# Attention heads in pairs on TensorE, and a weight ring of two slots beside them

## The chip, the core and the metric

The kernel runs on one NeuronCore of a Trainium2 chip, in one launch. The core has a matrix engine (TensorE; PE in the profile, with its weight loads as PEld), a vector engine (DVE), an activation engine (ACT), a general engine (POOL), a queue engine that here only issues DMA transfers (SP), an on-chip memory of 128 partitions (SBUF) and eight accumulator banks of 128 x 512 f32 (PSUM) that TensorE writes. The metric is the device time of one execution in microseconds. Three runs of the kernel before took 1537.32, 1537.51 and 1539.07 us (median 1537.51).

## The reference, cut to what matters

Two blocks in a row on a 512 x 1024 activation. The first mixes the sequence (a recurrence and a Fourier transform), then runs 16 experts. The second, whose middle is what changes here, is this:

```
h = rms_norm(x, norm_gain)
q, k, v, z_a, u, z_s, g_a, g_s = split(h @ w_in)         # 512 columns each, g_a and g_s 1024
g_a, g_s = g_a + gate_bias[:1024], g_s + gate_bias[1024:]
y_a = band_attention(q, k, v, rel_bias)                  # 8 heads of 64, chunk of 64, 8 chunks back
y_a = (y_a * silu(z_a)) @ w_attn_out
y_s = s5_ssm(u, ...)                                     # 32 groups, 64 complex states each
...                                                      # gelu, a gated linear unit, * silu(z_s), @ w_ssm_out
x = x + (sigmoid(g_a) * y_a + sigmoid(g_s) * y_s) @ w_out
```

With 512 positions every query sees all keys up to its own chunk, so a head is a lower triangle of 128 x 128 tiles: for the query tile q (0 to 3) the scores are 128 x 128(q+1), then bias, softmax over the row, and the product with the values.

## The kernel before, in words

Each engine has one instruction stream written out by hand; the order of the work is the order of the loops in the code, and semaphores tie the streams together. A weight matrix arrives in units of 1 MB. A unit goes through a chain: SP loads it into a slot of a ring (`load`, the slot by `slot_of`); ACT writes its rounded upper part into one of two other slots (`weights_hi`, `B2_HI`); DVE subtracts it in place, which leaves the lower part (`weights_lo`); TensorE then forms upper x lower, lower x upper and upper x upper products (`product`, `project`), and its last matmul of the unit counts up `unit_used`, which frees the slot.

The middle of the second block is a loop of `STEPS` = 12 steps `i`. Before it the units of u, q, k and v have been projected. Each step projects one unit of gate columns (two `project` calls of 24 matmuls each, into the banks of `gate{2i}` and `gate{2i+1}`). Behind them TensorE does what is left of step i, head by head, for the first `HEADS` = 8 steps:

- `head_scores(i+1)`: four matmuls with 64 rows (the head's 64 dimensions, q stationary, k moving), 384, 128, 256 and 512 columns wide. All matmuls of one head lie in the same half of the array's rows.
- `head_probs(i)`: ten transposes of 128 x 128 probability tiles through three banks.
- `ssm_out` (even steps) or `ssm_states` (odd steps): matmuls of the state space part, for group quarter c.
- `head_values(i)`: ten matmuls of 128 columns, the values stationary (64 columns, so half of the array's columns), the transposed probabilities moving.
- `ssm_tables` (even) or `ssm_lags` (odd): small matmuls for the tables of quarter c.

DVE in a step reads the score banks with scale and bias and takes the row maxima, multiplies the last head's result into `zaT`, scales the exponentials by the reciprocal sums, in even steps reads the lag rows and runs `states` (rotations and a scan), in odd steps builds `input_table`, and then makes the lower part of the next step's unit and finishes the silu of the gates. ACT takes the exponentials of head i, the upper part of the next unit, the tanh of the gates, and copies the transposed probabilities to SBUF (`pT`). POOL builds `output_table(c + 1)` as soon as `ssm_out(c)` has run, then writes y and the lag rows to memory and reads the lag rows back as `toep`, by DMAs that it issues itself.

The ring in this part has three slots (`B2_RING`, slots 4, 5 and 8); unit n waits for unit n - 3. The score banks are 0, 1 and 2, the state space banks 3, and four banks (4 to 7) take turns for gates, transposes and values. For scores of the first step the four matmuls of head 0 stand ahead of the loop.

Of the kernel before, what the change touches and what calls it, by code (L numbers as in the profile page):

```python
# [31 lines left out]
ALU = mybir.AluOpType  # L32
# [3 lines left out]
P = 128  # L36
# [16 lines left out]
HEADS, DH = 8, 64  # L53
NREL, CHUNK = 192, 64
# [26 lines left out]
B2_RING, B2_HI = (4, 5, 8), (9, 10)  # L81
MOE_END = B1_UNITS + NE * E_UNITS
# [48 lines left out]
def build(nc, x, cols_d, cst_d, wbd_d, w_in, dft_s, w_out, w_gate, w_up, w_down, gf_d, w_in2, relp,  # L131
          bc_d, w_glu, w_ao, w_so, w_out2, gfin_d, out, u_dram, y_dram, x_dram, l_dram):
    with ExitStack() as ctx:
# [91 lines left out]
        att = area("att", RING * UNIT, TT, S)  # L225
        relb = area("relb", ends["att"], HEADS, REL)
# [36 lines left out]
        ysT = kT  # L263

# [97 lines left out]
        SCORE_BANK, SSM_BANK = {3: 0, 2: 1, 1: 2}, 3  # L362
        for i in range(STEPS):
            if i == 0:
                for q in range(1, TT):
                    jobs.add(f"score0_{q}", SCORE_BANK[q])
            mine = (4, 5 + i % 2, 6 - i % 2, 7) if i < HEADS else (None,) * 4
            for n in range(2):
                jobs.add(f"gate{2 * i + n}", mine[n], M + 8 + i if n else None)
            if i + 1 < HEADS:  # L370
                for q in range(1, TT):
                    jobs.add(f"score{i + 1}_{q}", SCORE_BANK[q])
            if i < HEADS:
                for b in range(3):
                    jobs.add(f"probT{i}_{b}", mine[(2, 3, 0)[b]])
            if i % 2 == 0 and 2 <= i <= 2 * CT:
                jobs.add(f"ssm{i // 2 - 1}", SSM_BANK)
            if i % 2 == 1 and i < 2 * CT:
                jobs.add(f"state{i // 2}", SSM_BANK)
            if i < HEADS:  # L380
                jobs.add(f"pv{i}", mine[1])
            if i % 2 == 0 and i < 2 * CT:
                for n, name in enumerate(("st_re", "st_im")):
                    jobs.add(f"{name}_{i // 2}", mine[2 + n])
            if i % 2 == 1 and i < 2 * CT:
                jobs.add(f"lags_{i // 2}", mine[3])
            if i == HEADS - 1:
                jobs.turn = mine[0]
# [20 lines left out]
        def slot_of(unit):  # L409

            return unit % RING if unit < MOE_END else B2_RING[(unit - MOE_END) % RING2]

# [4 lines left out]
        def loaded(eng, unit):  # L417

            s = slot_of(unit)
            if unit < MOE_END:  # L420
                n = unit // RING + 1
            else:
                n = loads_b1[s] + (unit - MOE_END) // RING2 + 1
# [40 lines left out]
        def score_at(q):  # L464
# [1606 lines left out]
```

## Time and profile before

| | before |
|---|---|
| median of 3 runs | 1537.51 us |
| the profiled execution's own time | 1538.49 us |
| its span, first to last instruction | 1536.5 us |
| TensorE (PE) busy | 1407.3 us, 92% |
| DVE busy | 566.4 us, 37% |
| ACT busy | 315.6 us, 21% |
| POOL busy | 132.7 us, 9% |
| granted TensorE clock, mean | 0.989 of full speed |

The profile is one execution recorded on the chip. Busy time is the union of an engine's instructions; a busy TensorE need not be at its peak, since matmuls overlap and their ends are modelled. f32 matmuls are recorded as two instructions each, so that "x8" is four matmuls; transposes and the fp32r matmuls of the projections are one each. In a timeline row several instructions of one kind are merged, and the time in brackets is how long the engine was idle before the first, and for what. The experts take the span from about 220 to 1104 us; the loop of steps begins at 1210 us.

### The profile page before, as it was taken

What the parts mean: (1) busy time and instruction counts of PE and PEld (TensorE: products, weight loads), DVE (VectorE), ACT (ScalarE), POOL (GpSimd) and SP (SyncE); (2) the same over time, 40 slices, a digit from 0 to 9 for tenths busy, and PEclk for the clock granted to TensorE, in tenths of its full rate; (3) what the DMA queues carried; (4) which work ended last, traced back from release to release, by engine and by line L of the source; (5) the groups of instructions that cost most, each with busy time, mean ns of one, the idle gap of its engine ahead of it and who ended that gap; (6) DMA issues with size and microseconds to landing.
All of it is one profiled execution on the core that took longest, in us unless ns stands there. A gap on an engine that the chain in (4) does not pass through costs nothing.

```text
span 1536.5 us, 17099 instructions
## 1 busy us (share of the span) xinstructions
PE 1407.3 (92%) x6839; PEld 776.8 (51%) x6839; DVE 566.4 (37%) x1007; ACT 315.6 (21%) x501; POOL 132.7 (9%) x203
## 2 busy tenths in 40 slices
PE   7999699999998998988988988988799999999997
PEld 5878333443332332332332332333388888888875
DVE  6784501221120111111101201201389487755663
ACT  6582200010010010010000000000333333334332
POOL 1030000000000000000000000000123114451001
PEclk9999899999999999999999999999999999999999
DMA  9035599999999999999999999999755222225231
GB/s 330 1 107 222 219 390 425 428 428 428 427 428 430 429 428 428 428 430 428 428 427 429 430 427 428 428 430 429 280 176 139 83 73 79 70 88 185 83 110 55
DMA packets 67469, 465.19 MB, mean 303 GB/s; under 512 B 5472, under 2 KB 32352, under 8 KB 42720
## 3 DMA queue, kind: packets, MB, share of 16 engines
q1 hardware_dynamic: 63152, 454.71, 71.7%
q0 software_dynamic: 3984, 9.41, 2.4%
q8 instruction: 31, 0.51, 0.1%
q10 hardware_dynamic: 288, 0.45, 0.1%
q14 instruction: 14, 0.11, 0.0%
HBM read 457.76 MB, written 6.78 MB: 302 GB/s over the span
## 4 chain that ended last, share of the span: by engine, by line
PE 59%; DMA 34%; DVE 3%; ACT 2%; issue 1%; SPq 0%; POOL 0%; DVEq 0%; POOLq 0%; ACTq 0%
DMA wide<-in_w_down 23%; PE bank L788 14%; DMA early<-in_w_down 10%; PE bank L583 8%; PE bank L584 8%; PE bank L585 8%; PE bank L815 6%; PE bank L828 4%; PE bank L870 1%; PE bank L895 1%; PE bank L752 1%; PE bank L759 1%; ACT ring_r L1020 1%; DMA ring<-in_w_in 1%; PE bank L883 1%
## 5 line engine op out<-in xcount | busy, mean ns | idle before, releaser
L788 PE MATMUL bank<-wide,xinT 128*64 128x512 f32 x1376 | 306.9, 596 | 47.8 <-DMA wide<-in_w_up 26.9
L788 PEld LDWEIGHTS bank<-wide,xinT 128*64 128x64 f32 x1376 | 95.6, 137 | 257.3 <-issue 171.8
L1420 DVE SCALAR_TENSOR_TENSOR th<-th,bank 128x512 f32<-128x512 f32 x32 | 20.6, 684 | 432.8 <-ACT th L1155 432.8
L788 PE MATMUL bank<-early,xinT 128*64 128x512 f32 x672 | 150.5, 596 | 26.0 <-DMA early<-in_w_up 14.7
L815 PE MATMUL bank<-wide,actT 128*64 128x512 f32 x688 | 153.0, 594 | 3.7 <-issue 3.0
L583 PE MATMUL bank<-hT_lo,ring_r 128*128 128x512 f32 x352 | 139.9, 397 | 0.0
L585 PE MATMUL bank<-hT_hi,ring_r 128*128 128x512 f32 x352 | 137.1, 389 | 0.0
L584 PE MATMUL bank<-hT_hi,ring_r 128*128 128x512 f32 x352 | 137.1, 389 | 0.0
L1155 ACT ACTIVATE th<-bank 128x512 f32<-128x512 f32 x32 | 17.4, 595 | 516.1 <-PE bank L788 516.1
L788 PEld LDWEIGHTS bank<-early,xinT 128*64 128x64 f32 x672 | 45.9, 137 | 129.6 <-issue 79.0
L1417 DVE TENSOR_TENSOR ring_r<-ring,ring_r 128x2048 fp32r<-128x2048 f32 x38 | 88.3, 2324 | 43.5 <-ACT ring_r L1020 43.2
L815 PEld LDWEIGHTS bank<-wide,actT 128*64 128x64 f32 x688 | 55.4, 137 | 93.7 <-issue 80.0
L1417 DVE TENSOR_TENSOR xinT<-bank,cols 128x512 f32<-128x512 f32 x17 | 11.8, 691 | 223.2 <-PE bank L759 223.2
L1417 DVE TENSOR_TENSOR xres<-xres,bank 128x512 f32<-128x512 f32 x128 | 78.2, 681 | 7.5 <-PE bank L828 7.5
L1020 ACT ACTIVATE ring_r<-ring 128x2048 fp32r<-128x2048 f32 x38 | 72.5, 1910 | 33.3 <-PE bank L585 31.4
L1320 POOL TENSOR_SCALAR stat<-stat 128x1 f32<-128x1 f32 x4 | 1.3, 329 | 879.6 <-ACT hT L1175 879.5
L815 PE MATMUL bank<-early,actT 128*64 128x512 f32 x336 | 75.3, 595 | 2.1 <-issue 1.8
L583 PEld LDWEIGHTS bank<-hT_lo,ring_r 128*128 128x128 f32 x352 | 66.1, 188 | 16.2 <-issue 2.5
L584 PEld LDWEIGHTS bank<-hT_hi,ring_r 128*128 128x128 f32 x352 | 66.1, 188 | 14.3 <-issue 1.0
L585 PEld LDWEIGHTS bank<-hT_hi,ring_r 128*128 128x128 f32 x352 | 66.1, 188 | 14.0
L752 PE MATMUL bank<-nrm,sel 128*64 128x512 f32 x272 | 61.3, 592 | 0.8 <-issue 0.8
L828 PE MATMUL bank<-eo,gselT 64*128 64x512 f32 x256 | 60.8, 600 | 1.1
(336 smaller groups left out, 1705.6 us busy)
## 6 DMA issues: line engine op xcount, KB each, us to landing
wide<-in_w_gate SPq DMA_DIRECT2D x43, 2048.0 KB, 40.1
wide<-in_w_up SPq DMA_DIRECT2D x43, 2048.0 KB, 39.1
wide<-in_w_down SPq DMA_DIRECT2D x43, 2048.0 KB, 38.5
early<-in_w_gate SPq DMA_DIRECT2D x21, 2048.0 KB, 40.2
early<-in_w_up SPq DMA_DIRECT2D x21, 2048.0 KB, 39.2
early<-in_w_down SPq DMA_DIRECT2D x21, 2048.0 KB, 38.6
ring<-in_w_in SPq DMA_DIRECT2D x26, 1024.0 KB, 5.3
ring<-in_w_out SPq DMA_DIRECT2D x8, 1024.0 KB, 5.0
```

Source lines behind the costliest of these rows:

```text
L583: pe.matmul(dst, a[0], b[1], start=first, stop=False)
L584: pe.matmul(dst, a[1], b[0], start=False, stop=False)
L585: return pe.matmul(dst, a[0], b[0], start=False, stop=last)
L752: last = pe.matmul(bank[0][CAP * q:CAP * q + CAP, :], sel[:, t, :], nrm[:, t, 512 * q:512 * q + 512], start=(t == 0), stop=(t == TT - 1))
L759: last = pe.transpose(bank[0][:, j * P:(j + 1) * P], xg[:, 2 * P * (j // 2) + j % 2:2 * P * (j // 2 + 1):2], ident)
L788: last = pe.matmul(bank[1 + 2 * (m % 2) + q // 2][o:o + 64, :], xinT[:, k, :], w[:, i, q * 512:(q + 1) * 512], start=(k == 0), stop=(k == ...
L815: last = pe.matmul(bank[7][64 * n:64 * n + 64, :], actT[:, j // 2 * 4 + i, at:at + 64], w[:, i, n * 512:n * 512 + 512], start=(j == 0 and ...
L828: pe.matmul(bank[b][:, :], gselT[64 * n:64 * n + 64, t, :], eo[64 * n:64 * n + 64, :], start=True, stop=True).then_inc(bank_full[b], 1)
L1020: act_e.activation(hi_of(unit), used(unit, ring[slot_of(unit)]), ACT.Copy).then_inc(w_hi, 1)
L1155: act_e.activation(th[:, b, :], bank[1 + b][:, :], ACT.Tanh, scale=0.5).then_inc(tanh_ready, 1)
L1417: return dve.tensor_tensor(out_, a, b, op)
L1420: return dve.scalar_tensor_tensor(out_, a, s, b, op0, op1)
```

## The change

**Heads in pairs.** Heads 2p and 2p+1 are handled together. `pair_scores(p)` issues the eight score matmuls of both, alternating between the heads, so between rows 0 to 63 and rows 64 to 127 of the array; the six results that need a bank of their own go to six banks (`SCORE_TILES`). `pair_values(p)` has four matmuls per head instead of ten, 512, 384, 256 and 128 columns wide, alternating between the heads, so between the two column halves, into one bank. There is a second buffer `pT_b` for transposed probabilities, and probability tiles of the odd head lie in `att_b` and `att_c`; `att_c` and `pT_b` take the room of ring slot 8.

**Weight ring.** While slot 8 is taken, the units use only slots 4 and 5 (`B2_SLOTS`): from the unit of the sixth index on, unit n waits for unit n - 2. Slot 8 comes back at unit index 18, after the last pair's values.

**Order.** Scores of pair p+1, transposes, lags and values stand in the odd steps; tables, `ssm_out` and `ssm_states` in the even steps, in this order. DVE reads the scores of both heads and scales both in the even step, and runs `states` at the head of the odd step, its lag rows and input table at the tail. ACT makes the upper part of the next unit ahead of the exponentials in even steps, takes the eight exponentials there, and copies six pieces of transposed probabilities in the odd steps. The four reciprocals of a head are one. Banks are handed out anew. Nothing changes in what is computed.

The core of the diff (the rest is declarations and the same renaming on the other engines):

```diff
+B2_SLOTS = [4, 5, 8] * 2 + [4, 5] * 5 + [4, 5, 8] * 4 + [4, 5]
+SLOT8_BACK = 18
...
+        SCORE_TILES = [((0, 3),), ((1, 3),), ((0, 2), (0, 0)), ((1, 2), (1, 0)), ((0, 1),), ((1, 1),)]
...
-            mine = (4, 5 + i % 2, 6 - i % 2, 7) if i < HEADS else (None,) * 4
+            odd, (one, other) = i % 2, ((6, 7), (7, 6))[i // 2 % 2]
+                jobs.add(f"gate{2 * i + n}", ((5, one), (other, 5))[odd][n] if i < HEADS else None, M + 8 + i if n else None)
+                for a, b, at in ((0, 0, 0), (1, 0, 3), (0, 1, 1), (1, 1, 4), (0, 2, 2), (1, 2, other)):
+                    jobs.add(f"probT{2 * p + a}_{b}", at)
+                jobs.add(f"lags_{p}", one)
+                jobs.add(f"pv{p}", other)
...
+                    past = [k for k in range(v) if B2_SLOTS[k] == s]
+                    last = MOE_END + past[-1] if past else last_of[s // 2]
                     sp.wait_ge(unit_used, last + 1)
+                    if v == SLOT8_BACK:
+                        sp.wait_ge(*jobs.end(f"pv{PAIRS - 1}"))
...
+            def pair_scores(p):
+                for b in range(6):
+                    start(f"score{p}_{b}")
+                for a, q in ((0, 2), (1, 2), (0, 0), (1, 0), (0, 1), (1, 1), (0, 3), (1, 3)):
+                    b, at = SCORE_AT[a, q]
+                    nk, r = (q + 1) * P, 64 * a
+                    last = pe.matmul(bank[jobs.bank(f"score{p}_{b}")][:, at:at + nk], qT[r:r + 64, p, q * P:(q + 1) * P],
+                                     kT[r:r + 64, p, 0:nk], start=True, stop=True)
...
+            def pair_values(p):
+                b = start(f"pv{p}")
+                for kt in range(TT):
+                    at, n = (0, 4, 7, 9)[kt] * P, (TT - kt) * P
+                    for h in (2 * p, 2 * p + 1):
+                        r = 64 * (h % 2)
+                        was_read(pe, f"probT{h}_{min(kt, 2)}")
+                        last = pe.matmul(b[r:r + 64, S - n:S], v_s[:, kt, h * DH:(h + 1) * DH],
+                                         pTs[h % 2][:, at:at + n], start=(kt == 0), stop=(kt == TT - 1))
...
+            pair_scores(0)
+            ssm_tables(0)
             for i in range(STEPS):
...
-                if i + 1 < HEADS:
-                    head_scores(i + 1)
-                if i < HEADS:
-                    head_probs(i)
...
+                if i % 2 == 1 and i < HEADS:
+                    p = i // 2
+                    pair_probs(p)
+                    ssm_lags(p)
+                    pair_values(p)
+                    if p + 1 < PAIRS:
+                        pair_scores(p + 1)
+                if i % 2 == 0 and i <= HEADS:
+                    c = i // 2
+                    if 0 < c < CT:
+                        ssm_tables(c)
+                    if c:
+                        ssm_out(c - 1)
+                    if c < CT:
+                        ssm_states(c)
...
+                if i % 2 == 0 and i < HEADS:
+                    for a in range(2):
+                        scores_out(i // 2, a)
+                    for a in range(2):
+                        probabilities(i // 2, a)
+                if i % 2 == 1 and i < HEADS:
+                    states(i // 2)
                 weights_lo(M + 9 + i)
...
+                if i % 2 == 1 and i < HEADS:
+                    c = i // 2
+                    lag_rows(c)
+                    if c + 1 < CT:
+                        full(dve, f"st_im_{c}")
+                        input_table(c + 1)
```

Where it moves instructions, in three places.

TensorE, the end of an odd step (step 3, from the transposes on) in the kernel before. `att` holds probabilities, `st` and `ubuf` are the states' operands, `v_s` the values, `wc` and `bbd` the lags' operands:

```order
L883 MATMUL bank<-cst,att 128x128 [waits bank_read5,prob_ready]
L883 MATMUL bank<-cst,att 128x128 x3
L883 MATMUL bank<-cst,att 128x128 [waits bank_read7]
L883 MATMUL bank<-cst,att 128x128 x2
L883 MATMUL bank<-cst,att 128x128 [waits bank_read4]
L883 MATMUL bank<-cst,att 128x128 x2
L929 MATMUL bank<-ubuf,st 64x64 [waits bank_read7,bank_read3,bank_read6,u_in]
L929 MATMUL bank<-ubuf,st 64x64 x15
L895 MATMUL bank<-pT,v_s 64x128 [waits bank_read7,bank_read4,bank_read5,bank_read6]
L895 MATMUL bank<-pT,v_s 64x128 x9
L915 MATMUL bank<-wc,bbd 32x128 [waits bank_read7,wc_ready,bbd_ready]
L915 MATMUL bank<-wc,bbd 32x128 x7
```

TensorE after the change, from the last transposes of the odd step 3 to the end of its values:

```order
L917 MATMUL bank<-cst,att_c 128x128 [waits bank_read6]
L917 MATMUL bank<-cst,att_b 128x128 x2
L949 MATMUL bank<-wc,bbd 32x128 [waits bank_read7,wc_ready,bbd_ready]
L949 MATMUL bank<-wc,bbd 32x128 x7
L929 MATMUL bank<-pT,v_s 64x512 [waits bank_read0,bank_read6]
L929 MATMUL bank<-pT_b,v_s 64x512 [waits bank_read3]
L929 MATMUL bank<-pT,v_s 64x384 [waits bank_read1]
L929 MATMUL bank<-pT_b,v_s 64x384 [waits bank_read4]
L929 MATMUL bank<-pT,v_s 64x256 [waits bank_read2]
L929 MATMUL bank<-pT_b,v_s 64x256 [waits bank_read6]
L929 MATMUL bank<-pT,v_s 64x128 [waits bank_read2]
L929 MATMUL bank<-pT_b,v_s 64x128 [waits bank_read6]
```

The states' matmuls (L929 before) have moved out to the even step, the lags stand between transposes and values, and eight wide value matmuls replace ten narrow ones per head. The first of them waits for the bank (here bank 6) that also held the last piece of transposes.

ACT in the kernel before, the gates of the odd step 3 and what follows into step 4 (`ring_r` is the upper part of a unit, `zsT` a gate):

```order
L1226 ACTIVATE zsT<-bank 128x512 [waits bank_full4]
L1226 ACTIVATE zsT<-bank 128x512 [waits unit_used]
L1004 ACTIVATE pT<-bank 128x512 [waits bank_full5]
L1004 ACTIVATE pT<-bank 128x384 [waits bank_full7]
L1004 ACTIVATE pT<-bank 128x384 [waits bank_full4]
L1217 ACTIVATE att,stat<-att,stat 128x128 [waits max_ready]
L1217 ACTIVATE att,stat<-att,stat 128x256 [waits max_ready]
L1217 ACTIVATE att,stat<-att,stat 128x384 [waits max_ready]
L1217 ACTIVATE att,stat<-att,stat 128x512 [waits max_ready]
L1020 ACTIVATE ring_r<-ring_54 128x2048 [waits unit_used,ring_full5]
```

ACT after the change, the same gates of step 3:

```order
L1266 ACTIVATE zsT<-bank 128x512 [waits bank_full6]
L1266 ACTIVATE zsT<-bank 128x512 [waits unit_used]
L1039 ACTIVATE pT<-bank 128x512 [waits bank_full0]
L1039 ACTIVATE pT_b<-bank 128x512 [waits bank_full3]
L1039 ACTIVATE pT<-bank 128x384 [waits bank_full1]
L1039 ACTIVATE pT_b<-bank 128x384 [waits bank_full4]
L1039 ACTIVATE pT<-bank 128x384 [waits bank_full2]
L1039 ACTIVATE pT_b<-bank 128x384 [waits bank_full6]
L1055 ACTIVATE ring_r<-ring_54 128x2048 [waits unit_used,ring_full5]
L1258 ACTIVATE att_a,stat<-att_a,stat 128x128 [waits max_ready]
```

Six copies stand behind the gates where there were three, and the upper part of the next unit now stands ahead of the exponentials instead of behind them.

DVE, the end of `states` in the kernel before (an even step; `hbd` is what states() leaves, `ring_r` the lower part of a unit):

```order
L1417 TENSOR_TENSOR hbd<-tmp 64x4x63 [waits dve_step]
L1417 TENSOR_TENSOR hbd<-tmp 64x4x63
L1417 TENSOR_TENSOR ring_r<-ring_57,ring_r 128x2048 [waits w_hi,states_ready]
L1420 SCALAR_TENSOR_TENSOR zsT<-zsT,bank 128x512 [waits th_ready] x2
L1420 SCALAR_TENSOR_TENSOR att<-bank,relb 128x128 [waits bank_full1,bank_full4]
```

DVE after the change, the end of `states`, now in the odd step 3:

```order
L1457 TENSOR_TENSOR hbd<-tmp 64x4x63 [waits dve_step]
L1457 TENSOR_TENSOR hbd<-tmp 64x4x63
L1457 TENSOR_TENSOR ring_r<-ring_53,ring_r 128x2048 [waits w_hi,states_ready]
L1460 SCALAR_TENSOR_TENSOR zsT<-zsT,bank 128x512 [waits th_ready] x2
L1460 SCALAR_TENSOR_TENSOR lagsb<-diag,cols,bank 128x16 [waits l_out,bank_full7]
L1893 COPY lagsb<-bank 128x112
L1457 TENSOR_TENSOR wext<-pw_re,bc 128x512 [waits bank_full1]
```

The gates' products now wait behind `states` and the lower part of the unit, and the lag rows and the input table (`wext`) stand behind them.

## Rows read from the trace of the kernel before

**Rows 1.** Windows view, the stretch of the heads: busy us by engine, granted clock.

```profile
core 0: us, PE busy (x) PEld busy (x) DVE busy (x) ACT busy (x) POOL busy (x), PEclk, DMA share, GB/s
1212.40:1381.90 169.50, 168.61 (x1082) 138.37 (x1081) 122.95 (x280) 62.02 (x123) 62.47 (x96) 1.00 0.26 77
```

**Rows 2.** Timeline of PE: start, us, engine, line, operation, out<-in, count, idle before.

```profile
1210.11 2.39 PE L870 MATMUL bank<-kT,qT 64*128 64x384 f32 x8 [0.67 <-ACT v_s L1004]
1212.43 0.50 PE L583 MATMUL bank<-hT_lo,ring_r 128*128 128x512 f32 x1
...
1223.57 2.42 PE L870 MATMUL bank<-kT,qT 64*128 64x384 f32 x8
1225.93 1.31 PE L883 MATMUL bank<-cst,att 128*128 128x128 f32 x10
1228.13 2.37 PE L895 MATMUL bank<-pT,v_s 128*64 128x128 f32 x20 [0.89 <-ACT pT L1004]
1230.43 1.09 PE L905 MATMUL bank<-cst,wext 128*128 128x128 f32 x8
1231.28 0.48 PE L583 MATMUL bank<-hT_lo,ring_r 128*128 128x512 f32 x1
...
1245.94 1.15 PE L929 MATMUL bank<-ubuf,st 128*64 128x64 f32 x32
...
1249.21 0.64 PE L915 MATMUL bank<-wc,bbd 128*32 128x128 f32 x16
...
1264.39 0.39 PE L940 MATMUL bank<-hbd,wc 128*128 128x128 f32 x2
...
1268.06 2.40 PE L895 MATMUL bank<-pT,v_s 128*64 128x128 f32 x20
```

**Rows 3.** Timeline of PE: matmuls in two halves of the array.

```profile
1100.73 0.80 PE L828 MATMUL bank<-eo,gselT 64*128 64x512 f32 x2
1100.73 3.80 PE L828 MATMUL bank<-eo,gselT 64*128 64x512 f32 x16
...
1089.16 10.83 PE L815 MATMUL bank<-wide,actT 128*64 128x512 f32 x48
```

**Rows 4.** Timeline of DVE, first steps and one run of states().

```profile
1211.31 0.29 DVE L1420 SCALAR_TENSOR_TENSOR att<-bank,relb 128x128 f32<-128x128 f32 x1 [8.32 <-PE bank L870]
...
1215.25 0.15 DVE L1900 RECIPROCAL stat<-stat 128x1 f32<-128x1 f32 x1
...
1218.02 2.29 DVE L1417 TENSOR_TENSOR ring_r<-ring,ring_r 128x2048 fp32r<-128x2048 f32 x1 [0.72 <-ACT ring_r L1020]
...
1293.25 0.41 DVE L1417 TENSOR_TENSOR tmp<-bank,rotc 128x256 f32<-128x256 f32 x1
...
1300.43 2.29 DVE L1417 TENSOR_TENSOR ring_r<-ring,ring_r 128x2048 fp32r<-128x2048 f32 x1
```

**Rows 5.** Timeline of ACT.

```profile
1209.87 1.28 ACT L1217 ACT_TABLE_LOAD   x1
...
1232.09 0.40 ACT L1217 ACTIVATE att<-att,stat 128x128 f32<-128x128 f32 x1
...
1234.27 1.91 ACT L1020 ACTIVATE ring_r<-ring 128x2048 fp32r<-128x2048 f32 x1
...
1285.39 1.36 ACT L1004 ACTIVATE pT<-bank 128x512 f32<-128x512 f32 x3 [2.34 <-PE bank L883]
```

**Rows 6.** DMA issues, 1180 to 1390 us: KB each, us to landing.

```profile
ring<-in_w_in SPq DMA_DIRECT2D x12, 1024.0 KB, 5.2
```

**Rows 7.** Timelines of DVE and POOL: together, then each alone.

```profile
1182.57 1.55 DVE L1417 TENSOR_TENSOR wext<-pw_re,bc 128x512 f32<-128x512 f32 x1
1183.53 1.50 POOL L1365 TENSOR_TENSOR ybuf<-pw_in,bc 128x512 f32<-128x512 f32 x1
...
1235.01 0.69 DVE L1417 TENSOR_TENSOR wext<-pw_re,bc 128x512 f32<-128x512 f32 x1
1268.21 1.05 POOL L1364 TENSOR_TENSOR wc<-pw_re,bc 128x512 f32<-128x512 f32 x1 [8.02 <-PE bank L944]
```

More of the change, by code:

```diff
@@ L385, in build @@
[L385 to L388, printed above, removed]
+                jobs.add(f"gate{2 * i + n}", ((5, one), (other, 5))[odd][n] if i < HEADS else None, M + 8 + i if n else None)
+            if odd and i < HEADS:
+                p = i // 2
[4 more added lines that the diff above has]
+                if p + 1 < PAIRS:
+                    for b in range(6):
+                        jobs.add(f"score{p + 1}_{b}", b if b < 5 else one)
@@ L390, in build @@
+            if not odd and i <= HEADS:
+                c = i // 2
+                if 0 < c < CT:
+                    for n, name in enumerate(("st_re", "st_im")):
+                        jobs.add(f"{name}_{c}", n)
+                if c:
+                    jobs.add(f"ssm{c - 1}", 2)
+                if c < CT:
+                    jobs.add(f"state{c}", 3)
         last_units = [("ao", 0), ("glu", 0), ("glu", 4), ("ao", 4), ("so", 0), ("so", 4)]
@@ L872, in head_scores, with pair_probs @@
                     if q != 2:
[L873 to L877 removed]
+                        finish(f"score{p}_{b}", last)
+            def pair_probs(p):
+                pe.wait_ge(prob_ready, 2 * p + 2)
                 for piece, kts in enumerate(((0,), (1,), (2, 3))):
[L879 to L885 removed]
@@ new lines, in probabilities @@
+            def probabilities(p, a):
+                dve.wait_ge(exp_ready, TT * (2 * p + a + 1))
+                link(dve.reciprocal(one_over(a), sums_of(a)))
+                for q in range(TT):
+                    last = dve.tensor_scalar(att_tile(a, q), att_tile(a, q), one_over(a)[:, q:q + 1], None, ALU.mult)
+                last.then_inc(prob_ready, 1)
+            for i in range(STEPS):
+                if i % 2 == 0 and 0 < i <= HEADS:
+                    p, name = i // 2 - 1, f"pv{i // 2 - 1}"
+                    full(dve, name)
+                    was_read(dve, f"gate{p}")
+                    z = zaT[:, p, :]
+                    read(name, stt(z, bank[jobs.bank(name)][:, :], 0.5, z, ALU.mult, ALU.mult))
+                if i % 2 == 0 and i < HEADS:
+                    for a in range(2):
+                        scores_out(i // 2, a)
+                    for a in range(2):
+                        probabilities(i // 2, a)
+                if i % 2 == 1 and i < HEADS:
+                    states(i // 2)
```

214 lines of the change are left out of this document (88 added, 126 removed).

## The prediction

> **What bounds the kernel now.** I read the busy table first, then the stretch of the eight head steps in the windows view: TensorE is busy 168.61 of 169.50 us there at the full granted clock (1.00, the level of 2.4 GHz), DVE 122.95 us, ACT 62.02, POOL 62.47 [rows 1]. So the end of this stretch is set by what TensorE issues, and other engines count only where they would now make it wait. Then TensorE's timeline shows what each group costs, read from start to start [rows 2]: a unit's projection 11.14 us (1212.43 to 1223.57), the scores of one head 2.36 (1223.57 to 1225.93), ten transposes about 1.25, the values of one head 2.30 (1228.13 to 1230.43), tables 0.85, states 1.0 (busy 1.15 with the overlap), lags 0.57 (busy 0.64), `ssm_out` 3.67 (1264.39 to 1268.06). The only wait in the loop is 0.89 us of the first values for ACT's copies.
>
> **Scores.** The eight matmuls of a pair (16 instructions) stay, 2560 columns in all, 2 x 2.36 = 4.72 us today. Scatter matmuls elsewhere in this trace already alternate between row halves (L828, 64*128): eight of 512 columns take 3.80 us, and the first two instructions start inside 0.3 us, one in each half, since both together last 0.80 [rows 3]. That is 0.475 us for 512 columns, or 2.37 us for a pair's 2560. Saved: 2.35 x 4 = 9.4 us. Bounds: nothing saved, if rows do not pair at K = 64 with these widths, and 10.2 at the bare column rate of a perfect pair (2560 columns x 4 passes / 2 / 2.4 GHz = 2.13 us).
>
> **Values.** 2 x 2.30 = 4.60 us today. The experts' down projection alternates column halves (L815): 24 matmuls of 512 columns in 10.83 us, 0.45 each [rows 3]. A pair's 2560 columns: 2.26 us. Saved 2.34 x 4 = 9.4 us. Bounds: nothing, if these widths do not pair, and 9.9 at the bare column rate.
>
> **The 0.89 us** of the first values goes: the next values stand behind 20 transposes and the lags. But the same row prices a new wait. In step 0 the values start 2.20 us after the first transpose (1225.93 to 1228.13), behind three copies of 1.36 us together [rows 2, 5]. Now the bank that the values of a pair write also held the last piece of transposes, so their very first matmul waits for all six copies: 2.20 + 1.36 = 3.56 us after the first transpose, while TensorE would be there after 2 x 1.25 + 0.57 = 3.07. Cost 0.5 x 4 = 2.0 us (bounds 0 and 1.0 each). Behind that wait stand the next pair's scores, and behind these DVE.
>
> **First step.** Unit index 9 now shares slot 5 with the last unit of v, so its load begins only at 1209.4 (1210.11 less 0.67 idle) and lands 5.2 us later [rows 6], 1214.6. ACT then makes its upper part (1.91), 1216.6, and only behind it loads the exponential table (1.28) and takes eight exponentials (2.18 a head, 1232.09 to 1234.27): 1222.3 [rows 5]. DVE's scores of two heads (3.94 each, from 1211.31) are done at 1219.2; it scales the second head (2.05 today, about 1.5 with one reciprocal for four) until 1223.8, and the lower part (2.3) is ready at 1226.1 [rows 4]. TensorE: scores to 1212.43, tables 0.85, projection 11.14, states 1.0: 1225.4. It waits 0.7 us. Bounds 0, and 3 if the load takes 2.3 us longer than the median.
>
> **Later steps.** With everything paired an even step is 11.14 + 0.85 + 3.67 + 1.0 = 16.65 us of TensorE, an odd one 11.14 + 2.5 + 0.57 + 0.5 + 2.26 + 2.35 = 19.3; together 36.0 against 40.0. DVE has in an even step 0.7 (product with the gate) + 7.9 + 3.0 + 2.3 + 1.3 (two gates) = 15.2, in an odd one 7.2 (`states`, 1293.25 to 1300.43) + 2.3 + 1.3 + 0.3 + 4.2 (six table products of 0.69) = 15.3 [rows 4, 7]. The lower part for the next step is ready 14.0 us into an even step of 16.65: no wait. Ring of two slots: a unit is freed 11.14 into step i, lands after 5.2 and is split in 4.2; it is used no sooner than 25 us after. No wait.
>
> **A collision that the move of `states` makes.** POOL's output table starts when `ssm_out` ends; until now DVE had exponentials to scale then. Now `states` starts 1.0 us behind it. Where both engines multiply SBUF operands, one DVE product takes 1.55 us against 0.69 alone, and POOL's 1.50 against 1.05 [rows 7]: they take turns. The Trainium skill says the same in "SBUF — State Buffer", section "Who interferes with whom": the port pair is an exclusive lock, also for a DVE operation with two SBUF inputs. POOL then has some 6 us of table work left when `states` leaves its four PSUM reads, so I stretch `states` from 7.2 to about 12 us (bounds 7.2 and 13.5). In step 3 the gates' products stand behind it and the lower part: the first is done at 0.2 + 12 + 2.3 + 0.7 = 15.2 into the step, and the last piece of transposes takes over its bank at 11.14 + 2.1 = 13.3. Of these 2 us part is in the copies' wait already: cost 1.5 (bounds 0 and 2.5). In steps 5 and 7 ACT reads the gates, and `states` has room until 19.3; step 1 has no table beside it.
>
> **Sum**, against the profiled execution's own 1538.49 us: -9.4 - 9.4 - 0.9 + 2.0 + 0.7 + 1.5 = -15.5, so 1523.0. The median of the runs shown is 1.0 below that execution: 1522.0. Past the heads the rest hangs on TensorE and keeps its distances; I count nothing there.
>
> **Rivals.**
> - *The passes are issued strictly in turn.* An f32 matmul is two instructions. If a head's second pass must start before the other head's first, unequal widths leave gaps: with 128 columns of one instruction as a unit (0.107 us), the scores take 26 units in place of 20 and the values 24, +1.07 us a pair, +4.3 in all: 1526.3. Against it: two instructions start inside the first 0.8 us of L828, where that order would leave the second half idle for 0.43 [rows 3]; but equal widths are all that the rows show. 12%.
>  The Trainium skill, "TensorE: Matmul & The Clock Gate", Part 3, calls matmuls strict FIFO in start and end; by that rule the time would be this rival's.
> - *DVE becomes the pace.* 30.5 us of own work in 36.0, plus 5 of lock in two of four pairs, leaves nearly nothing. If the lock also stretches the input table or the score reads, each of three pairs loses 2 to 3 us more: about 1529. The window's 122.95 us of busy DVE speaks for it, the 2.6 us of slack in even steps against. 17%.
> - *Row halves do not overlap here.* +9.4: 1531.4. Rows 3 speak against. 4%.
> - *Neither collision nor copies cost anything.* 1522.0 - 3.5 = 1518.5. 10%.
> - *The other side: the weight chain becomes the bound.* With two slots the upper part stands ahead of the exponentials in even steps. From the moment a slot is freed, load + 1.9 + 4.4 + 1.5 + 2.3 must fit in 8.2 + 16.65 = 24.8 us; that decides once a load takes over 14.7 us, and the kernel is slower than before only if each of four takes some 4 us longer than that, 18.6: about 1539. The 5.2 us of twelve loads speak against. 3%.
>
> **How the numbers follow.** Forecast 54%, its own range 1520 to 1525. Down to 1517 takes in the lossless case, up to 1530 the issue order and most of a pacing DVE; what is left out is under 2 in 10. A difference of 0.2% (3 us) is about what a measurement can tell. Faster 95%, within 0.2% 2%, slower 3%.
>
> **What would show it.** In the trace after: score groups of 16 instructions in 2.4 us (3.0 would be the issue order, 4.7 no overlap), value groups of 16 in 2.3; TensorE idle before the values for ACT's copies, four times 0.5; before step 1's projection for the lower part, 0.7; in step 3's last transposes for the gate product; `states` stretched to 12 us wherever POOL's table runs, not in step 1. I am wrong if the loop is not 15 us shorter, or if TensorE waits for the lower part in later even steps.

## The result, and the profile after

The changed kernel takes 1521.81 us (median of 4 runs, 1520.61 to 1522.71), the kernel before, run beside it, 1538.13 us (1537.32 to 1539.07): ratio 0.9893, 95% interval 0.9876 to 0.991. The forecast was 1522.0. Two of the edited kernels below each had one execution at a much lower granted clock (2394.93 us at 0.56 of full speed, 2660.85 us at 0.82), and these two are left out of their medians, ranges and ratios.

The experts, which stand ahead of the loop, end at a slightly different time in each execution (1102.6 to 1105.2 us over the thirteen profiled ones), and that shifts all that follows. So the two profiled executions (1538.49 and 1521.82 us of their own time) are compared over the stretch from the first scores to the projection that follows the last `ssm_out`: 1210.11 to 1381.90 before, 171.8 us, and 1210.15 to 1365.40 after, 155.25 us. Page of the kernel after, busy time, share and instructions:

```profile
PE 1388.6 (91%) x6743; PEld 759.7 (50%) x6743; DVE 563.9 (37%) x979; ACT 315.7 (21%) x501; POOL 129.5 (9%) x203
```

Windows view of the kernel after, the stretch and what follows it; the columns are those of [rows 1]:

```profile
1210.15:1365.40 155.25, 152.33 (x993) 122.65 (x993) 121.61 (x255) 63.92 (x125) 58.95 (x96) 1.00 0.32 95
1365.40:1520.00 154.60, 143.86 (x626) 116.93 (x625) 86.02 (x100) 50.70 (x65) 9.52 (x22) 0.98 0.32 110
```

All of the difference lies in the first row. What follows takes 154.6 us before too (1381.90 to the span's end at 1536.5), and in the profiled execution of every run below. DVE, ACT and POOL are busy within 4 us of what they are in [rows 1]; TensorE has 16 us less. DVE is now busy 78% of the stretch against 73%.

TensorE's timeline after, which answers to [rows 2] (first step, then the end of step 1, then the same place in step 3; the name behind `bank<-` is the tile that is multiplied, `pT` the even head and `pT_b` the odd one):

```profile
1210.15 2.43 PE L903 MATMUL bank<-kT,qT 64*128 64x384 f32 x16 [1.25 <-ACT v_s L1039]
1212.51 1.09 PE L939 MATMUL bank<-cst,wext 128*128 128x128 f32 x8
1213.95 0.47 PE L614 MATMUL bank<-hT_lo,ring_r 128*128 128x512 f32 x1 [0.34 <-ACT st L1039]
...
1225.04 1.15 PE L963 MATMUL bank<-ubuf,st 128*64 128x64 f32 x32
1226.12 0.50 PE L614 MATMUL bank<-hT_lo,ring_r 128*128 128x512 f32 x1
...
1237.14 0.60 PE L917 MATMUL bank<-cst,att_a 128*128 128x128 f32 x4
...
1239.42 0.64 PE L949 MATMUL bank<-wc,bbd 128*32 128x128 f32 x16
1240.50 0.64 PE L929 MATMUL bank<-pT,v_s 128*64 128x512 f32 x1 [0.44 <-ACT pT_b L1039]
1240.51 0.64 PE L929 MATMUL bank<-pT_b,v_s 128*64 128x512 f32 x1
...
1242.81 2.43 PE L903 MATMUL bank<-kT,qT 64*128 64x384 f32 x16
1245.16 0.50 PE L614 MATMUL bank<-hT_lo,ring_r 128*128 128x512 f32 x1
...
1272.82 0.60 PE L917 MATMUL bank<-cst,att_a 128*128 128x128 f32 x4
...
1275.92 0.33 PE L917 MATMUL bank<-cst,att_c 128*128 128x128 f32 x1 [1.08 <-DVE zsT L1460]
...
1277.05 0.64 PE L929 MATMUL bank<-pT,v_s 128*64 128x512 f32 x1
```

Read from start to start: a pair's scores take 2.35 us (1242.81 to 1245.16), its values 2.31 (1240.50 to 1242.81), and the first value matmuls of the two heads start 0.01 us apart. Those groups took as long for one head before. The waits that are left, TensorE after, 1200 to 1500 us (line, waited for: us in all, times, longest):

```profile
PE bank L929 <- ACT pT_b L1039: 1.5, 3, 0.5
PE bank L903 <- ACT v_s L1039: 1.2, 1, 1.2
PE bank L917 <- DVE zsT L1460: 1.1, 1, 1.1
PE bank L614 <- DVE ring_r L1457: 0.6, 1, 0.6
PE bank L614 <- ACT st L1039: 0.3, 1, 0.3
```

The 0.6 for `ring_r` lies behind the stretch and is in the kernel before as well. These are idle times, counted from the modelled end of the instruction before; what a wait costs is read from starts, and comes out somewhat larger. DVE after, the end of step 0 and `states` in step 1, then `states` in step 3:

```profile
1223.32 2.28 DVE L1457 TENSOR_TENSOR ring_r<-ring,ring_r 128x2048 fp32r<-128x2048 f32 x1
1225.52 1.28 DVE L1460 SCALAR_TENSOR_TENSOR zaT<-zaT,bank 128x512 f32<-128x512 f32 x2
1226.72 0.42 DVE L1457 TENSOR_TENSOR tmp<-bank,rotc 128x256 f32<-128x256 f32 x1
...
1228.16 0.76 DVE L1457 TENSOR_TENSOR tmp<-tmp 128x256 f32<-128x256 f32 x2
1228.95 0.29 DVE L1867 TENSOR_TENSOR_SCAN tmp<-mag,tmp 128x64 f32<-128x64 f32 x1
...
1233.91 2.29 DVE L1457 TENSOR_TENSOR ring_r<-ring,ring_r 128x2048 fp32r<-128x2048 f32 x1
...
1261.92 0.42 DVE L1457 TENSOR_TENSOR tmp<-bank,rotc 128x256 f32<-128x256 f32 x1 [2.77 <-PE bank L963]
...
1263.38 2.44 DVE L1457 TENSOR_TENSOR tmp<-tmp 128x256 f32<-128x256 f32 x2
1265.85 1.03 DVE L1867 TENSOR_TENSOR_SCAN tmp<-mag,tmp 128x64 f32<-128x64 f32 x1
...
1272.98 2.29 DVE L1457 TENSOR_TENSOR ring_r<-ring,ring_r 128x2048 fp32r<-128x2048 f32 x1
1275.19 1.28 DVE L1460 SCALAR_TENSOR_TENSOR zsT<-zsT,bank 128x512 f32<-128x512 f32 x2
```

POOL after, its table beside that second run (last row: its DMAs follow):

```profile
1260.88 1.05 POOL L1404 TENSOR_TENSOR wc<-pw_re,bc 128x512 f32<-128x512 f32 x1 [11.62 <-PE bank L978]
...
1264.41 1.12 POOL L1407 TENSOR_TENSOR wc<-pw_in,bc 128x512 f32<-128x512 f32 x1
...
1266.82 1.34 POOL L1409 TENSOR_TENSOR wc<-wc,relb 128x512 f32<-128x512 f32 x1
...
1270.51 4.20 POOL L1431 DMA_DIRECT2D y_scratch<-ybuf  x8
```

`states` takes 7.19 us with POOL idle (1226.72 to 1233.91) and 11.06 beside the table (1261.92 to 1272.98). Its four reads of PSUM take 0.42 either way; the two products of SBUF operands behind them take 2.44 instead of 0.76. The gate's product starts only at 1275.19, and the last piece of transposes, which takes over the bank that it reads, stands still for it. In steps 5 and 7, which also have a table beside them, `states` takes 11.05 us as well, and TensorE waits for none of it.

### The profile page after: what moved, and what is told of

Read it like the earlier page. It is cut to its first block, busy times and chain, and to the rows that moved or that the text cites. A ratio compares the mean times of both kernels' runs of the same rounds, so it can differ in the third digit from the quotient of the medians.

```text
span 1520.0 us, 16865 instructions
## 1 busy us (share of the span) xinstructions
PE 1388.6 (91%) x6743; PEld 759.7 (50%) x6743; DVE 563.9 (37%) x979; ACT 315.7 (21%) x501; POOL 129.5 (9%) x203
## 4 chain that ended last, share of the span: by engine, by line
PE 56%; DMA 35%; DVE 5%; ACT 2%; issue 1%; SPq 0%; POOL 0%; DVEq 0%; POOLq 0%; ACTq 0%
DMA wide<-in_w_down 23%; PE bank L819 14%; DMA early<-in_w_down 11%; PE bank L614 8%; PE bank L616 8%; PE bank L615 8%; PE bank L846 6%; PE bank L859 4%; PE bank L783 1%; PE bank L790 1%; ACT ring_r L1055 1%; DMA ring<-in_w_in 1%; PE bank L903 1%; PE bank L929 1%; DVE ring_r L1457 1%
## 5 line engine op out<-in xcount | busy, mean ns | idle before, releaser
L819 PEld LDWEIGHTS bank<-wide,xinT 128*64 128x64 f32 x1376 | 95.6, 137 | 257.2 <-issue 171.8
L819 PE MATMUL bank<-early,xinT 128*64 128x512 f32 x672 | 150.5, 596 | 25.5 <-DMA early<-in_w_up 15.2
```

Of the source, the lines that this page charges most:

```text
L819: last = pe.matmul(bank[1 + 2 * (m % 2) + q // 2][o:o + 64, :], xinT[:, k, :], w[:, i, q * 512:(q + 1) * 512], start=(k == 0), stop=(k == ...
```

## The experiments

Each run is the kernel after with one edit, unless said. "Stretch" is that from the first scores to the projection behind the last `ssm_out` in its profiled run (155.2 after); times are medians, beside runs of the kernel before on the same chip. The edits are shown cut to their core.

| run | time, us (range) | ratio to before, 95% | stretch, us |
|---|---|---|---|
| scores head by head | 1525.4 (1524.55 to 1526.57) | 0.9913 (0.9897 to 0.993) | 159.2 |
| values head by head | 1527.45 (1526.57 to 1528.59) | 0.993 (0.9911 to 0.9946) | 161.5 |
| unequal widths in turn | 1523.31 (1521.68 to 1524.08) | 0.9902 (0.9885 to 0.9918) | 156.4 |
| narrow value matmuls, paired | 1522.67 (1522.54 to 1523.52) | 0.9904 (0.9884 to 0.9924) | 155.8 |
| another bank for the values | 1521.35 (1520.38 to 1521.41) | 0.9886 (0.9866 to 0.9905) | 153.7 |
| gate's product first | 1520.25 (1519.55 to 1521.16) | 0.9883 (0.9867 to 0.99) | 154.4 |
| POOL's tables left out | 1520.49 (1519.64 to 1522.13) | 0.9889 (0.9873 to 0.9906) | 154.3 |
| before, ring of two slots | 1538.34 (1536.8 to 1539.89) | 1.0004 (0.9995 to 1.0014) | 172.4 (before 171.8) |
| first step reordered | 1520.43 (1519.3 to 1521.11) | 0.9892 (0.9876 to 0.9909) | 153.8, tables ahead of it |
| three edits together | 1518.71 (1518.3 to 1520.0) | 0.9882 (0.9865 to 0.9898) | 152.3, tables ahead of it |
| and both gates first | 1517.65 (1516.27 to 1517.79) | 0.9863 (0.9847 to 0.988) | 151.3, tables ahead of it |

The experts' shift, up to 2.6 us between two executions, is as large as many of the effects, so these are read from the stretch. Each stretch is one execution; what speaks for it is that groups with the same work agree between the traces, the nine projections together within 0.15 us. Two traces are the exceptions, each with 0.5 us more in one projection, and they are named below.

**Scores head by head.** Is it the turn between row halves that saves?

```
-for a, q in ((0, 2), (1, 2), (0, 0), (1, 0), (0, 1), (1, 1), (0, 3), (1, 3)):
+for a, q in ((0, 2), (0, 0), (0, 1), (0, 3), (1, 2), (1, 0), (1, 1), (1, 3)):
```

> The changed kernel, with the scores of a pair issued head by head (all four of rows 0 to 63, then all four of rows 64 to 127) instead of alternating. Theory (the gain of the scores comes from alternating row halves, not from grouping two heads): a score group takes 4.4 to 4.7 us instead of 2.36, four groups, so the kernel is 8.5 to 9.4 us slower than the changed one, 1530 to 1531. Rival (the array starts the second head's matmuls early whatever the order, through a reorder window): 2.4 us a group and no change, 1522.

**Values head by head.** The same question for column halves.

```
-for kt in range(TT):
-    for h in (2 * p, 2 * p + 1):
+for h in (2 * p, 2 * p + 1):
+    for kt in range(TT):
```

> The changed kernel, with the four value matmuls of one head before the four of the other instead of alternating. Theory (the gain of the values is the pairing of column halves): a value group takes 4.3 to 4.5 us instead of 2.31; +8 to +8.8 us, of which the waits for ACT's copies, hidden then, give back nothing since the first matmul waits for the last copy anyway: 1530. Rival (the gain comes from fewer and wider matmuls, four per head instead of ten): at most the 10% of overhead of narrow ones is at stake, so 2.4 us a group and 1522.

Both came out between the two cases. Timeline of TensorE, the score group of step 1 with scores head by head:

```profile
1244.42 3.40 PE L903 MATMUL bank<-kT,qT 64*128 64x384 f32 x16
```

And the value group of step 1 with values head by head:

```profile
1239.29 1.93 PE L929 MATMUL bank<-pT,v_s 128*64 128x512 f32 x5 [0.44 <-ACT pT_b L1039]
1240.85 0.64 PE L929 MATMUL bank<-pT_b,v_s 128*64 128x512 f32 x1
1241.06 0.49 PE L929 MATMUL bank<-pT,v_s 128*64 128x256 f32 x2
1241.33 0.59 PE L929 MATMUL bank<-pT_b,v_s 128*64 128x512 f32 x1
...
1243.15 2.43 PE L903 MATMUL bank<-kT,qT 64*128 64x384 f32 x16
```

The odd head's first instruction stands ninth in the program. It starts at 1240.85, when five instructions of the even head have started, and overtakes the other three. Read instruction by instruction, it is the same in all four value groups (the fifth starts 1.55 us into the group, the ninth 1.56), and in the score groups of the other run the ninth again starts with the fifth, there 0.97 us into the group (0.94 in the first). The time differs and the place doesn't, so what fits these runs is a look-ahead counted in instructions, about four (two f32 matmuls), for one whose half is free. The value group takes 3.86 us (1239.29 to 1243.15): 1.56 until then, and 2.3 for the odd head. The score group takes 3.33 us (the projection starts at 1247.75), 0.98 more than in turn, which is when the fifth instruction of the even head starts. Times four: 1.55 x 4 = 6.2 us (stretch +6.3) and 3.9 (stretch +3.9). The edit shows what taking turns adds over that look-ahead; without any overlap the group would be the 4.7 us of two heads in [rows 2].

**Unequal widths in turn.** Heads still alternate, but a 512 wide matmul stands beside a 256 wide one. Does a half wait until the other's matmul has started or ended?

```
-for a, q in ((0, 2), (1, 2), (0, 0), (1, 0), (0, 1), (1, 1), (0, 3), (1, 3)):
+for a, q in ((0, 3), (1, 2), (0, 2), (1, 0), (0, 0), (1, 1), (0, 1), (1, 3)):
```

> The changed kernel with the score matmuls alternating between the row halves but in unequal widths: 512 with 384, 384 with 128, 128 with 256, 256 with 512. What is disputed is how far ahead the array issues. If pairs go in lockstep (strictly in turn), the group is the sum of the wider of each pair, 13 against 10 units, 3.05 us instead of 2.36, +0.7 x 4 = +2.8 us. If it looks some instructions ahead, as the head-by-head order suggests (3.4 us a group instead of 4.7: the second head's matmuls overlapped the last four instructions of the first), the halves run on their own and the group is 2.4 to 2.6 us: +0 to +0.8 us.

```profile
1244.17 2.74 PE L903 MATMUL bank<-kT,qT 64*128 64x512 f32 x16
```

2.74 beside 2.43 in the kernel after, or 2.66 beside 2.35 from start to start: 0.3 us a pair, 1.2 for four, stretch +1.1. That is neither case: the lockstep would be 3.05, and halves on their own were given 2.6 at most. The look-ahead fills over half of the gaps.

**Narrow value matmuls, paired.** The change also made ten matmuls into four. Here the ten of 128 columns are back, still alternating between heads.

```
-for kt in range(TT):                      # 512, 384, 256, 128 columns
-    for h in (2 * p, 2 * p + 1):
+...                                      # waits for all six copies first
+for q in range(TT):
+    for kt in range(q + 1):               # 128 columns each
+        for h in (2 * p, 2 * p + 1):
```

> The changed kernel with the values in ten matmuls of 128 columns per head as before the change, but alternating between the heads and so between the column halves. Theory (pairing alone carries the values' gain; width is worth little): 2.3 to 2.5 us a group against 2.31, +0 to +0.8 us in all. Rival (weight loads of 64 columns for every 128 columns of work do not hide twice over when both halves run): 3 us or more a group, +3 us.

```profile
1240.68 0.29 PE L932 MATMUL bank<-pT,v_s 128*64 128x128 f32 x1 [0.53 <-ACT pT_b L1042]
...
1243.01 2.43 PE L903 MATMUL bank<-kT,qT 64*128 64x384 f32 x16
```

2.33 us against 2.31, from start to start. The whole gain of the values is the pairing, none the width. The stretch is 0.55 us longer all the same: the value groups give 0.1 of it, and 0.4 stands ahead of them, where this edit puts the waits for all six copies together (the first values start 1.18 us after the lags in step 1, against 1.09).

**Another bank for the values.** The lags take bank 5, and the values the bank that the lags had, which holds no transposes.

```
-jobs.add(f"lags_{p}", one)
+jobs.add(f"lags_{p}", 5)
-jobs.add(f"pv{p}", other)
+jobs.add(f"pv{p}", one)
```

(The sixth bank of the next scores goes from `one` to `other`.)

> The changed kernel with three banks traded: lags in bank 5, values in the bank the lags had, the sixth score bank of the next pair where the last transposes were. Theory (TensorE's idle of 0.44, 0.52 and 0.52 us ahead of the values of pairs 0, 2 and 3 is the bank shared with the last transposes, whose copy is the sixth on ACT): the idle is gone, -1.5 us. Rival (it is the data: the values need all copies soon anyway, so the wait only moves behind the first value matmuls): the idle reappears between value matmuls and the time stays within 0.3 us.

No wait for `pT_b` is left, and the stretch is 1.5 us shorter: by starts, the values come 0.5 to 0.6 us sooner in steps 1, 5 and 7, and 0.1 later in step 3. There the 1.08 for `zsT` stays, and the lags now wait 0.14 behind it.

**Gate's product first.** DVE multiplies the first gate of an odd step ahead of the lower part of the unit, not behind it.

```
 states(i // 2)
+gate_end(2 * i)          # odd steps, i < 4
 weights_lo(M + 9 + i)
```

> The changed kernel with DVE's product for the first gate of steps 1 and 3 ahead of the lower part of the weight unit instead of behind it. Theory (the 1.08 us that TensorE stands in the transposes of step 3 is this product, queued behind the stretched states and the lower part): the stall goes, -1.1 us, states stays stretched at about 11 us. Rival (the bank is held by something else): no change.

**POOL's tables left out.** The output tables of quarters 1 to 3 are not built, so the state space output of these quarters is not the reference's.

```
+if c:
+    pool.memset(scratch[:, 0:8], 0.0).then_inc(wc_ready, 1)
+    return
```

> The changed kernel with POOL's output tables for the quarters 1 to 3 left out (the tables of quarter 0 are used for all, so the state space part is not the reference's for them); the rest is untouched. Theory (DVE's states and POOL's table take turns at SBUF, which stretches states from 7.2 to 11.1 us in step 3 and makes the 1.1 us stall in the transposes): states takes 7.2 us in every odd step, the stall of step 3 is gone and a wait of 0.4 for ACT's sixth copy takes its place, as in the other pairs: the stretch from the first scores to the last state space output is 0.9 us shorter, 154.3 against 155.2. Rival (states is late because TensorE hands it over late, or DVE waits for something else): states and the stall stay.

Timeline of DVE, step 3 without the table:

```profile
1262.96 0.42 DVE L1460 TENSOR_TENSOR tmp<-bank,rotc 128x256 f32<-128x256 f32 x1 [2.76 <-PE bank L963]
...
1264.42 0.76 DVE L1460 TENSOR_TENSOR tmp<-tmp 128x256 f32<-128x256 f32 x2
...
1270.16 2.29 DVE L1460 TENSOR_TENSOR ring_r<-ring,ring_r 128x2048 fp32r<-128x2048 f32 x1
```

`states` is back at 7.2 us, and the stall in step 3 is gone. Both edits shorten the stretch by 0.9. The transposes of step 3 take 1.3 us less from start to start (2.27 in place of 3.58), and 0.4 comes back, as the fourth wait for `pT_b`, which the stall had hidden, appears in step 3. Moving one product costs nothing that shows and gives as much as taking the table away.

**Before, with the ring of two slots.** The kernel before with `B2_SLOTS` in place of `B2_RING` and nothing else.

```
-return unit % RING if unit < MOE_END else B2_RING[(unit - MOE_END) % RING2]
+return unit % RING if unit < MOE_END else B2_SLOTS[unit - MOE_END]
```

> The kernel before with the changed ring alone: units 6 to 17 of the second block use slots 4 and 5 only, heads singly as before. Theory (a slot is freed 25 us ahead of its use, and load plus the two parts need 10): nothing lost, the stretch stays 171.8 us (within 0.3). Rival (the two slots cost something that the changed kernel hides or pays, such as a load colliding with the POOL transfers or the last v unit's upper part late): 1 to 4 us longer, with TensorE waiting for ring_r at the head of steps.

The times of 10 runs show no difference (at most 0.14% by the interval). The stretch is 0.6 us longer, twice what was allowed for, and not where the ring would show: up to the projection of step 8 it takes 157.3 us in both (1210.11 to 1367.39, and 1208.88 to 1366.20), without a wait for `ring_r`. The projection of step 8 then takes 11.50 us instead of 11.01, with 0.3 us in which TensorE waits for nothing that the profile names; why stays open. The room for `att_c` and `pT_b` cost nothing that these runs can tell.

**First step reordered.** TensorE does `ssm_tables(0)` ahead of the first scores, where it waits for the last copy of v, and ACT takes the exponentials of step 0 ahead of the upper part.

```
+ssm_tables(0)
 (waits for q, k and v)
 pair_scores(0)
-ssm_tables(0)
```

> The changed kernel with the first tables (ssm_tables(0)) ahead of the first scores, before the waits for v, and in step 0 the exponentials ahead of the upper part of the next unit. Theory (0.6 us between the tables and the first gates is the bank shared with the tables' copy; the tables can also fill the 1.2 us of waiting for the last v copy): the first step's projection starts 1.0 to 1.4 us sooner after the end of v than the 5.0 us of the changed kernel, and TensorE does not wait for the lower part in step 1; -1.0 to -1.4 us. Rival (DVE's chain of scores, exponentials and lower part then ends last in step 0, since it was only 0.5 us ahead): the gain ends up as a wait of 0.5 to 1 us at the head of step 1, -0.3 us.

```profile
1207.54 1.04 PE L933 MATMUL bank<-cst,wext 128*128 128x128 f32 x8
1208.90 2.43 PE L897 MATMUL bank<-kT,qT 64*128 64x384 f32 x16 [0.33 <-ACT st L1038]
```

The last copy of v starts at 1207.73 here, and the scores 1.17 us after; in the kernel after it is 1208.94 and 1.21. So the tables cost nothing now, as they run while the scores would wait anyway, and the 1.4 us from the start of `ssm_tables` (1212.51) to the projection (1213.95) are gone: 0.85 of work and 0.59 of waiting. What ACT's part of the edit does is not told apart from this; TensorE did not wait for the lower part in step 1 without it either.

**Three edits together** (bank, gate, first step).

> The traded banks, the earlier gate product and the mended first step together. If they add: -1.5 (values no longer wait) -1.1 (no stall in step 3) -1.2 (first step) = -3.8 us, 1518.0 us. If one wait only uncovers another: DVE, with 30.5 to 34.5 us of work in periods that shrink from 35.8 to 35.2, becomes the last to arrive in steps 3 to 5 and 1 to 2 us of it come back: 1519.5.

```profile
1274.35 0.64 PE L943 MATMUL bank<-wc,bbd 128*32 128x128 f32 x16 [1.44 <-DVE zsT L1462]
```

The edits don't add up: 1.5, 0.9 and 1.4 would be 3.8 us, and the stretch is 3.0 shorter (155.2 to 152.3). The lags now use bank 5, which also holds the second gate of step 3, and wait for its product, behind the lower part: 1.44 us. The bank edit had only moved the place where step 3 waits for DVE.

**And both gates first.** In step 3 alone both products stand ahead of the lower part.

```
-early = i % 2 == 1 and 2 * i < 2 * CT
+early = (i % 2 == 1 and 2 * i < 2 * CT) + (i == 3)
```

> The three edits together with one more: in step 3 both products with the gates stand ahead of the lower part of the unit, not only the first. Theory (each wait seen in step 3 is for whatever DVE has queued behind states() and the 2.3 us of the lower part): gate 7's product is then done about 0.7 us after gate 6's, near 1274.5 to 1275 in the trace, when TensorE comes to the lags at about 1274.3; the 1.44 us of the lags for zsT shrink to 0.4 or less. The stretch from the first scores to the last ssm_out goes from 152.3 to about 151.2, the time from 1518.7 to about 1517.5. Rival: the lower part, now 1.3 us later, is needed by the next projection or holds back DVE's lag rows and table, and a wait of the same size stands elsewhere in step 3 or at the start of step 4: stretch 152.3, time 1518.7.

All waits of TensorE from 1200 to 1500 us in this run:

```profile
PE bank L614 <- DVE ring_r L1459: 0.6, 1, 0.6
PE bank L897 <- ACT st L1038: 0.4, 1, 0.4
PE bank L614 <- DVE att_b L1462: 0.2, 1, 0.2
```

The stretch is 151.3 us where 151.2 was expected, the time 1517.65 us, some 4 us below the kernel after and the fastest of all runs here. The sum came out right with another split, though. The 1.44 of step 3 is gone whole (1.5 by starts), and 0.5 comes back in step 4: its projection takes 11.51 us instead of 11.02, since the bank of its second gate held the last tile of the pair's scores, and DVE has read it only at 1284.00, just ahead of that gate's first matmul at 1284.06. That is the 0.2 for `att_b`, and part of what the rival expected: with the other waits gone, DVE is the last to arrive there. The ratio to before is 0.9863 (0.9847 to 0.988).

## Why the prediction was right, step by step

The number was right, and the two large terms were right for their reasons. Of the small ones one was absent, one unforeseen, and they nearly cancel. The hit to 0.2 us is luck in part: the two profiled executions differ by 16.7 us and the stretch by 16.5, where 15.5 was forecast. All measured terms below are differences of sums over the stretch, from start to start of the groups.

| term | on record | measured |
|---|---|---|
| scores, four pairs | -9.4 | 9.44 - 18.80 = -9.4 |
| values, four pairs | -9.4 | 9.22 - 18.42 = -9.2 |
| the old wait for `pT` | -0.9 | -0.9 |
| values wait for six copies | +2.0 in steps 1, 3, 5, 7 | +1.7 in steps 1, 5, 7 |
| step 3, gate's product | +1.5 | +1.4 |
| step 1 waits for the lower part | +0.7 | 0 |
| step 0 waits for the tables' copy | none | +0.6 |
| twenty transposes in a row | none | -0.6 |
| projections, tables, states with other neighbours | none | -0.5, +0.1, +0.3 |
| stretch | -15.5 | -16.5 (the lines are rounded) |

**Scores and values.** Rows 3 gave 0.475 and 0.45 us for 512 columns of a pair; a pair with mixed widths came out 0.02 us below the 2.37 and 0.05 above the 2.26 worked out from them. The head by head runs show that the turn is what brings it, the narrow one that width is not.

**The copies.** The mechanism and its size, 0.5 to 0.6, were right: the copies of step 1 end 3.3 us after the first transpose, the values start at 3.36. In step 3 the stall stands ahead of it and takes it in. From first transpose to first value matmul it is 3.36 us in step 1 and 4.23 in step 3 (1272.82 to 1277.05), and 2.85 in the last experiment, where nothing waits (1270.61 to 1273.46): 0.5 and 1.4. The prediction had 2.0 for step 3 (0.5 + 1.5) and `states` at 12 us; it was 11.06, so the gate's product was done 14.1 us into the step (1275.87 less 1261.81) and not 15.2, and the loss came out 0.6 smaller.

**Twenty transposes in a row** take 2.28 us (1237.14 to 1239.42), not the 2 x 1.25 that I took over from groups of ten. In the kernel before two groups of ten take 1.24 + 1.15, or 2.4, so that a pair saves a little over 0.1 us.

**The collision** was where it was predicted and not in step 1, where POOL is idle, and the run without the tables shows its cause. In "SBUF — State Buffer", section "Who interferes with whom", the Trainium skill says that a DVE instruction with two SBUF inputs contends with a GpSimd instruction that reads SBUF, and that one with a single SBUF input, outside the two-port modes, does not; the trace agrees: 0.76 to 2.44 us for two products of SBUF tiles, 0.42 and 0.42 for the reads of PSUM. A scan of 64 columns takes 1.03 instead of 0.29 as well.

**Step failed: the first step.** I had TensorE wait 0.7 us for the lower part at 1226.1. It was ready at 1223.32 + 2.28 = 1225.6, since the load ran from 1208.94 to 1214.0, not from 1209.4 to 1214.6, and ACT could start the upper part at 1214.18, straight behind its copies of `st`; and TensorE came at 1226.12, as it had lost 0.6 us before. That loss is the step I missed. ACT after, first step:

```profile
1208.94 0.38 ACT L1039 ACTIVATE v_s<-bank 128x256 f32<-128x256 f32 x1 [2.49 <-PE bank L616]
1213.21 1.08 ACT L1039 ACTIVATE st<-bank 128x512 f32<-128x512 f32 x2 [3.88 <-PE bank L939]
```

`gate0` now takes over bank 5, which held a table of `ssm_tables`, and its first matmul at 1213.95 waits for ACT's copy of it, 0.6 us after 1213.36, where the tables (1212.51 and their 0.85) are done. I had listed the banks of the values, and not those of the tables. The reordered first step takes this wait away.

**Rivals.** *Strictly in turn* (12%) is out: the halves start 0.01 us apart, the odd head's first instruction ahead of the even head's second (1240.51 and 1240.98), and even unequal widths cost 0.3 us a pair, not the 0.7 of a lockstep. "TensorE: Matmul & The Clock Gate", Part 3, of the Trainium skill says that matmuls keep program order in start and end. Here that does not hold between column halves: with values head by head the ninth instruction starts at 1240.85, the sixth at 1241.06. The measurement decides. *DVE becomes the pace* (17%): it is busy 78% of the stretch, but TensorE waits for it 1.1 us in all (1.4 by starts); `states` beside the table was stretched, and no score reads. The rival's sum had 5 us of lock in two of four pairs; the trace has 3.9 in three of them, steps 3, 5 and 7. In the last experiment, 4 us shorter, DVE does arrive last in step 4. *Neither costs anything* (10%): both cost, together 3.1 us. *Halves don't overlap* (4%) and *the weight chain* (3%): neither; the ring alone gives a ratio of 1.0004.

**Ahead of the first scores,** outside the stretch, TensorE now waits 1.25 us where it waited 0.67. The last copy of v ends at 1209.33, and the scores start 0.83 after, against 0.26 before (1209.85 to 1210.11). What lies between are instructions in TensorE's own queue that only wait for semaphores, up to two each. In both kernels they start about 0.106 us apart and take 51 ns each, none longer, so no other engine is late there. Two stand between the copy and the first weight load before (1209.89 and 1210.00), seven after (1209.37 to 1210.05), since `pair_scores` asks for all six banks ahead of its first matmul. By line, after and before (the one of `was_read` in each is not shown; count, ns, first to last start):

```profile
L586 PEldq EVENT_SEMAPHORE  x6: 51/51/51, 1209.5 to 1210.0; - x6
L555 PEldq EVENT_SEMAPHORE  x1: 51/51/51, 1210.0 to 1210.0; - x1
```

All eleven kernels with pairs have seven there and start the scores 0.78 to 0.83 us behind the copy; the one with only the ring has two and 0.25. No run takes these waits apart, so the cause is read from the traces and not tested. The 0.57 us were missing in the prediction, and the two time totals hide them: the experts happened to end 0.53 us earlier in the profiled execution of the kernel after (1104.01 and 1104.54).

## What to carry over

Two heads of 64 fit the array side by side in either direction, and the gain is full only when their matmuls alternate in the program; head by head, the look-ahead brings over half of it for the scores and a third for the values. When a bank changes hands, write down for each first matmul whose copy it now waits for, in the first step too: here three of the four new delays were banks (the sixth copy's, the gate's, the tables'), and the fourth the waiting instructions ahead of the first scores. Mending the banks one by one moved a wait to the next user of DVE's queue, and half a microsecond of it was still there in the fastest run. A product that frees a bank belongs ahead of a long operation that nobody waits for.

## What the runs showed of the hardware

- TensorE starts an instruction in a free half ahead of earlier ones whose half is busy: with two heads one after the other, the ninth starts with the fifth, ahead of three, in all eight groups. A pair's scores take 3.3 us head by head, 2.35 in turn, 4.7 with no overlap; values 3.86, 2.31 and 4.6.
- In a pair, 20 f32 matmuls of 128 columns take 2.33 us and 8 of up to 512 take 2.31, with the same columns in all.
- DVE's scan of 64 columns is stretched by POOL as well: 1.03 and 1.31 us beside POOL's products of 512 columns, 0.26 to 0.29 alone.
- In TensorE's queue an instruction that only waits for semaphores takes about 0.106 us even when they are there: 0.25 us from copy to first matmul with two of them, 0.78 to 0.83 with seven.
